# The attention output projection as seven block products per pair half, instead of eight

## The reference

```python
    o = ...                      # attention output of all heads, (544 tokens, 1024)
    yp = o @ w_out               # w_nsa_out, 1024 x 1024: the output projection
    xp = xp + rmsnorm(yp, norm_g[i, 1])
    fp, bp = conv_ffn(rmsnorm(xp, norm_g[i, 2]), zbuf, w_ffn_up[i], ...)

def rmsnorm(x, g):
    y = x * lax.rsqrt(jnp.mean(x * x, axis=-1, keepdims=True) + RMS_EPS)
    return y * g
```

## Time and profile before

| | |
|---|---|
| median of three runs | 2114.21 us |
| the profiled execution | 2110.09 us, span 2108.3 us, clock 0.999 |
| PE busy | 2070.4 us (98%), PEld (weight loads, beside PE) 1635.3 us |
| DVE / ACT / POOL busy | 1316.8 / 638.5 / 264.1 us |

### The profile page before, as it was taken

The page is one execution under the profiler, slowest core; times in us unless marked ns, Lnnn a source line. Parts: engine busy times, 40 slices in busy tenths (PEclk is TensorE's granted clock), DMA queues, the critical chain, the costliest instruction groups (busy, mean ns, idle before and its releaser), DMA issues.

```text
span 2108.3 us, 30368 instructions
## 1 busy us (share of the span) xinstructions
PE 2070.4 (98%) x11142; PEld 1635.3 (78%) x11142; DVE 1316.8 (62%) x3052; ACT 638.5 (30%) x1462; POOL 264.1 (13%) x499
## 2 busy tenths in 40 slices
PE   8999999999999999999999999999999999999998
PEld 7556777777788888888888775778888888888887
DVE  5257996672877776778323784655877777675223
ACT  3016886562332222221001321543322222220002
POOL 1002000000022222221000100410222222210001
PEclk9999999999999999999999999999999999999999
DMA  9228106994222222222221334252222222212223
GB/s 221 59 62 272 53 2 161 278 255 79 81 80 80 80 80 80 81 84 90 87 80 60 134 82 100 77 157 86 83 81 85 88 88 91 88 62 80 80 80 117
DMA packets 207493, 214.14 MB, mean 102 GB/s; under 512 B 40530, under 2 KB 192314, under 8 KB 206834
## 3 DMA queue, kind: packets, MB, share of 16 engines
q1 hardware_dynamic: 203330, 194.44, 32.0%
q0 software_dynamic: 4016, 17.75, 2.5%
HBM read 198.56 MB, written 21.93 MB: 105 GB/s over the span
## 4 chain that ended last, share of the span: by engine, by line
PE 91%; DVE 3%; SPq 2%; ACT 2%; DMA 2%; issue 1%; DVEq 0%; ACTq 0%
PE PS L2981 58%; PE PS L1847 3%; PE PS L2813 2%; PE PS L1639 2%; PE PS L2792 2%; PE PS L1718 2%; PE PS L750 2%; PE PS L822 2%; PE PS L737 2%; PE PS L2943 2%; PE PS L770 2%; PE PS L1591 2%; PE PS L2822 1%; PE PS L2716 1%; DMA arena<-in_cache_nsa_kv 1%
## 5 line engine op out<-in xcount | busy, mean ns | idle before, releaser
L2981 PE MATMUL PS<-HT,ring 128*128 128x272 f32 x1536 | 373.4, 393 | 2.3 <-DVE HT L3759 2.3
L2981 PE MATMUL PS<-arena,ring 128*128 128x272 f32 x1392 | 341.6, 392 | 0.0
L2981 PEld LDWEIGHTS PS<-HT,ring 128*128 128x128 f32 x1536 | 291.4, 190 | 63.2 <-ACT arena L3271 1.8
L2981 PEld LDWEIGHTS PS<-arena,ring 128*128 128x128 f32 x1392 | 264.3, 190 | 54.5
L3339 ACT ACTIVATE arena<-arena,CB,CW 128x560 f32<-128x560 f32 x128 | 109.1, 854 | 378.1 <-DVE arena L3819 313.9
L2981 PE MATMUL PS<-arena,CONST 128*128 128x272 f32 x768 | 191.7, 392 | 0.0
L2981 PE MATMUL PS<-arena 128*128 128x272 f32 x768 | 191.4, 392 | 0.0
L3834 DVE SCALAR_TENSOR_TENSOR arena<-arena,CW 128x560 f32<-128x560 f32 x256 | 187.3, 788 | 0.0
L2981 PEld LDWEIGHTS PS<-arena,CONST 128*128 128x128 f32 x768 | 145.9, 190 | 30.1
L2981 PEld LDWEIGHTS PS<-arena 128*128 128x128 f32 x768 | 145.8, 190 | 30.0
L4033 POOL COPY arena<-arena 128x16 f32<-128x16 f32 x128 | 50.9, 398 | 622.3 <-DVE arena L3819 524.7
(11 more groups left out here) (544 smaller groups left out, 3339.1 us busy)
## 6 DMA issues: line engine op xcount, KB each, us to landing
ring<-in_w_ffn_up SPq DMA_DIRECT2D x64, 1024.0 KB, 6.7
ring<-in_w_ffn_down SPq DMA_DIRECT2D x32, 1024.0 KB, 5.2
ring<-in_cache_nsa_kv SPq DMA_DIRECT2D x128, 128.0 KB, 5.9
arena<-in_cache_nsa_kv SPq DMA_DIRECT2D x56, 256.0 KB, 7.1
ring<-in_w_ml_in SPq DMA_DIRECT2D x12, 1024.0 KB, 6.3
arena<-in_cache_nsa_win SPq DMA_DIRECT2D x16, 512.0 KB, 6.7
out_nsa_win_sample<-in_cache_nsa_win POOLq DMA_DIRECT2D x8, 1016.0 KB, 17.4
ring<-in_w_nsa_in SPq DMA_DIRECT2D x6, 1024.0 KB, 5.8
```

The source lines that it names most:

```text
L2981: last = mm(PS[:, bank, 0:HALF], lhs[:, k, :], rhs(k), start=(first and k == 0), stop=(done and k == 3))
```

## The change

Seven of the eight pair halves of the projection are computed as seven block products. A pair half is a 2 x 2 block product: two output blocks by two quarters of 136 tokens, over two halves of the input channels. The pair half that is left plain is (half 0, pair 0), by `out_part` as before. What was 14 blocks of 8 matmuls of 272 columns is now 7 groups (half 0 with pairs 1, 2, 3, half 1 with pairs 0 to 3) of 7 products of 4 matmuls of 136 columns, in the order 1, 2, 5, 6, 7, 3, 4.

```diff
         def out_bank(idx, m):
-            return (m + 2 * (idx == 1)) % 4
+            return 2 + m % 2 if idx == 1 else m % 4
...
+            def out_group(gi):
+                h, p = A_GROUPS[gi]
+                arrived(W_AO + p)
...
+                for i, j in enumerate(A_PRODUCTS):
...
+                    n = 7 * gi + i
+                    if n in (1, 2):
...
+                    elif n < 4:
+                        pe.wait_ge(s_z, Z0[1] + (2 if n == 0 else 1))
+                    else:
+                        out_read(n - 4)
+                    if j in (5, 6, 7, 3):
+                        pe.wait_ge(s_su, ASU + A_SUMS.index((p, {5: "s1", 6: "s2", 7: "s3", 3: "s4"}[j])) + 1)
+                    if j in (5, 6, 7, 4):
+                        pe.wait_ge(s_xs, AXS + 4 * h + {5: 1, 6: 2, 7: 3, 4: 4}[j])
+                    for k in range(4):
+                        last = mm(out_place(gi, j), lhs[:, k, :], rhs[:, k, :], start=(k == 0), stop=(k == 3))
...
+                    if gi == 3 and j == 7:
+                        z_sum(1, 0, 4)
+            def out_product(ready):
+                for gi in range(7):
...
+                    out_group(gi)
+                    if gi == 5:
+                        x_gathered(2, 0, 6)
...
+            def attention_out():
+                out_chunk(1, M_AO0, 0, 0)
+                out_chunk(1, M_AO0, 0, 1)
+                out_first(0)
+                out_fifth(0)
+                for gi in (1, 2, 3):
+                    out_first(gi)
+                    out_squares(gi - 1)
+                    out_fifth(gi)
+                root(1, 0, 4)
...
+                out_first(6)
+                out_squares(5)
+                root(2, 0, 6)
+                out_fifth(6)
+                out_squares(6)
+                root(1, 1, 5)
...
+            def out_early():
+                out_tokens(0)
+                out_sums(1, ("s3", "s1", "s2", "s4"))
+            def before_first_ffn():
...
+                out_tokens(1)
+                out_adds(0, A_ADDS)
+                gather(1, 0, range(1, 2))
+                out_sums(0, ("s3", "s1"))
+                out_sums(2, ("s3", "s1", "s2", "s4"))
+                out_adds(1, A_ADDS)
...
+                gather_joined(2, 0, range(5, 8))
+                out_adds(5, A_ADDS[4:7])
+                inverse(2, 0, half(0))
+                scaled(2, 0)
+                gather(1, 1, range(4, 6))
+                out_adds(6, A_ADDS)
+                gather(1, 1, range(6, 7))
+                weight_sums(0, 0, 0)
+                inverse(1, 1, half(1))
```

More of the change, by code:

```diff
@@ L1170, in nsa_act, with nsa_dve @@
                     heads_copy(p)
-        def nsa_dve(dve, chain):
+        def nsa_dve(dve, chain, out_early):
             v = nc.vector
@@ L1457, in nsa_dve @@
                 else:
+                    out_early()
                     heads_copy(p)
@@ L2931, in out_product, with out_read @@
+            def out_read(n):
+                gi, i = divmod(n, 7)
+                j = A_PRODUCTS[i]
+                if j in (1, 5):
+                    pe.wait_ge(s_ac, AAC + 2 * gi + (1 if j == 1 else 2))
+                else:
+                    pe.wait_ge(s_ev, out_added(gi, A_READER[j]))
+            def out_product(ready):
+                for gi in range(7):
+                    if gi == 3:
                         for s, n in ready:
                             pe.wait_ge(s, n)
[L2933 to L2949, removed]
@@ L3239, in out_chunk, with out_first, out_fifth, out_squares @@
                                      scale=NG[:, 8 * idx + m:8 * idx + m + 1]).then_inc(s_z, 1)
+            def out_first(gi):
+                act.wait_ge(*out_done(gi, 1))
+                h, p = A_GROUPS[gi]
+                copy(ZT[:, 2 * p + 1, quarters(h)[1]], out_place(gi, 1)).then_inc(s_ac, 1)
+            def out_fifth(gi):
+                act.wait_ge(*out_done(gi, 5))
+                h, p = A_GROUPS[gi]
+                copy(ZT[:, 2 * p + 1, quarters(h)[0]], out_place(gi, 5)).then_inc(s_ac, 1)
+            def out_squares(gi):
+                h, p = A_GROUPS[gi]
+                for c in range(2):
+                    m = 2 * p + c
+                    act.wait_ge(s_ev, out_added(gi, ("c12", "c21")[c]))
+                    nc.scalar.activation(squared(1)[:, m, half(h)], ZT[:, m, half(h)], ACT.Square).then_inc(s_sqz, 1)
+                    nc.scalar.activation(ZT[:, m, half(h)], ZT[:, m, half(h)], ACT.Copy,
+                                         scale=NG[:, 8 + m:9 + m]).then_inc(s_z, 1)
+            def attention_out():
[8 more added lines that the diff above has]
+                root(1, 0, 4)
+                out_first(4)
+                out_squares(3)
+                out_fifth(4)
+                x_squares(2, 0, range(0, 3))
+                out_first(5)
+                x_squares(2, 0, range(3, 8))
+                out_squares(4)
+                out_fifth(5)
+                out_first(6)
[4 more added lines that the diff above has]
+                root(1, 1, 5)
+                x_squares(2, 1, range(8))
+                root(2, 1, 5)
+                state_copies(0)
             def out_copies(idx, m0):
@@ L3503, in joined_gained, with joined_runs @@
                 joined_runs(idx, cols, (6, 7))
-            def joined_runs(idx, cols, plain=()):
+            def joined_runs(idx, cols, plain=(), between=None):
                 runs = ((0, 2), (2, 4), (4, 6), (6, 7), (7, 8))
@@ new lines, in out_sums @@
+            def out_sums(p, names):
+                a11, a12, a21, a22 = slot_blocks((W_AO + p) % RING)
+                w = A_WS[p]
+                dve.wait_ge(s_w[(W_AO + p) % RING], loaded(W_AO + p))
+                for x in names:
+                    out, a_, b_, op = {"s3": (w["s3"], a11, a21, ALU.subtract), "s1": (w["s1"], a21, a22, ALU.add),
+                                       "s2": (w["s2"], w["s1"], a11, ALU.subtract),
+                                       "s4": (w["s4"], a12, w["s2"], ALU.subtract)}[x]
+                    if x in ("s2", "s4"):
+                        dve.wait_ge(s_su, ASU + A_SUMS.index((p, {"s2": "s1", "s4": "s2"}[x])) + 1)
+                    v.tensor_tensor(out, a_, b_, op).then_inc(s_su, 1)
@@ new lines, in out_adds @@
+            def out_adds(gi, names):
+                h, p = A_GROUPS[gi]
+                qa, qb = quarters(h)
+                z1, z2, u3 = ZT[:, 2 * p, :], ZT[:, 2 * p + 1, :], A_U3[gi % 2]
+                first, fifth = z2[:, qb], z2[:, qa]
+                for x in names:
+                    out, a_, j = {"c11": (z1[:, qa], first, 2), "u2": (first, first, 6), "u4": (z1[:, qb], first, None),
+                                  "u3": (u3, first, 7), "c22": (first, u3, None), "c12": (z1[:, qb], z1[:, qb], 3),
+                                  "c21": (fifth, u3, 4)}[x]
+                    if j is not None:
+                        dve.wait_ge(*out_done(gi, j))
+                    if x == "c11":
+                        dve.wait_ge(s_ac, AAC + 2 * gi + 1)
+                    elif x == "u4":
+                        dve.wait_ge(s_ac, AAC + 2 * gi + 2)
+                    if x in ("u4", "u3", "c22", "c12", "c21"):
+                        dve.wait_ge(s_ev, out_added(gi, {"u4": "u2", "u3": "u2", "c22": "u3", "c12": "u4", "c21": "c22"}[x]))
+                    v.tensor_tensor(out, a_, fifth if j is None else out_place(gi, j), ALU.add).then_inc(s_ev, 1)
@@ L3956, in _ @@
             project()
-            nsa_dve(dve, chain)
+            nsa_dve(dve, chain, out_early)
             dve.wait_ge(s_kvo, 16 * (1 + 2 * NB))
-            before_ffn(0)
+            before_first_ffn()
             ffn(0)
```

87 lines of the change are left out of this document (78 added, 9 removed).

## The result

| | before | changed |
|---|---|---|
| median | 2113.75 us (5 runs) | 2122.52 us (5 runs, 2120.80 to 2124.09) |
| ratio | | 1.0044, 95% interval 1.0033 to 1.0055 |
| profiled execution | 2110.09 us, span 2108.3 | 2124.09 us, span 2122.3 |
| mean granted clock of it | 0.999 | 0.995 |

The change makes the kernel slower by 8.8 us by the medians. The time of 2122.52 lies in the forecast range, 2.5 us above the forecast of 2120.0; the change itself is 3.0 us above the forecast +5.8. The two profiled executions are 14.0 us apart, more than the medians: the changed one happened to have more of the half clock, also in places that the change doesn't touch. So what follows takes waits and spacings from the profiles, and totals from the runs.

The account below looks back on a forecast made before the run. PE, 91% of the last chain, bounds the kernel. Start 498.5, columns 45.5, norms 1.4 and waits end at 555.6 against 550.79, +4.8; with 0.85 behind, +5.8 taken: 2120.0 us on median 2114.2, range 2114.5 to 2125.0.

Parts of the forecast that it names:

- The columns: PE's 392 records of 136 columns at 0.116 us spacing take 45.5 us, saving 5.8 us at most.
- The rival of 0.12 to 0.125: Weight loads set the projection's record spacing, or the half clock comes: 2121 to 2124 us; chance 20% together.
- The start: PE's first product waits for ACT's scaled copy in bank 3 and starts at 498.5: 2.0 us lost.
- The eight early sums: `out_early` on DVE, some 5.4 us, fits into its idle time from 490.30 to 496.6 and costs nothing.
- The early waits: PE waits for DVE's sums before product 5: 1.7 us in group 1, 0.9 in group 2, 0.1 one product later.
- Group 5, and `x_gathered`: PE waits 0.7 us for `c12` before group 5's product 5, then 1.5 us for DVE before `x_gathered`.
- The last group: In group 6, product 3 waits for `c11` behind root, reciprocal, `scaled` and gathers: 5.1 us lost.
- The rival of half the waits: Waits are half as long, 2.6 us or less in group 6: +1 to +3, about 2116 us; chance 24%.
- After the last product: Half 1's mean square first needs an add and a gather: done 2.05 us after the last product, 0.85 more.
- The sum of the path: Start, columns, norms and waits through the projection, plus the later mean square: +5.8 us in all.
- The clock: PE's clock may halve in group 6's long wait: 1 to 2 us more, kept in the range, not the sum.
- the slow rival: Projection products slower than 0.116 us spacing, or the clock falls: 2121 to 2124 us; chance 20%.

Follow-up runs that it names:

- E1: Changed kernel with its products rotated by one bank, so the first goes to a free bank; 2120.27 us, ratio to before 1.0034.
- E8: Kernel before with one wait added: TensorE's third block waits until ACT has copied the second; 2115.09 us, ratio 1.0010.
- E10: E6 with `x_gathered`, and ACT's root behind it, one block later; 2108.36 us, ratio to before 0.9982.
- E3: Changed kernel with the weight sums of pairs 2 and 3 formed earlier on DVE, between the adds of the group before; 2119.14 us, ratio to before 1.0028.
- E2: Changed kernel, last group reordered: ACT's root right behind group 5, adds spread between reciprocal and pairs of `scaled`; 2117.40 us, ratio to before 1.0025.
- E4: Changed kernel with ten unread matmuls of 272 columns in a free bank before product 3 of the last group; 2121.02 us, ratio to before 1.0041.
- E7: Changed kernel with only `c11`, the last group's first add, moved ahead of the second reciprocal on DVE; 2119.96 us, ratio to before 1.0036.
- E5: Changed kernel with the edits of E1, E2 and E3 together; 2113.40 us, ratio to before 1.0002.
- E6: Block products only for half 0's three pair halves, half 1 plain as before, banks and sums as in E1 and E3; 2110.78 us, ratio to before 0.9990.
- E9: E10 with a fourth group of block products, (half 1, pair 0); 2109.16 us, ratio to before 0.9988.
- E11: Kernel before with only `x_gathered` and the root behind it one block later, no block products; 2110.90 us, ratio 0.9998.

## Why the prediction was right, and where it was short

- **The columns.** The spacing of 0.116 that it took from 129 columns is what was measured. It lies on the slope of the columns and above the 0.111 of loads alone, so nothing shows the weight loads setting it. The rival of 0.12 to 0.125 fell.
- **The start.** 2.0 lost, measured 1.91 in the bracket; E1 removes it and E8 alone makes it. Right. The eight early sums cost nothing, as forecast: DVE does them from 492.71 to 498.10, ahead of the heads' turn, and the start of the path in E10 shows no loss.
- **The early waits.** 1.7, and 0.9 and 0.1 one product later: measured 1.47, 0.74. The names of the releasers on PE are "issue" here; that they are DVE's sums is shown by E3, where the sums come sooner and the waits are gone. Right, each about 0.2 too high.
- **Group 5, and `x_gathered`.** 0.7 and 1.5: measured 0.40 and 1.40. Right in kind, the first 0.3 too high. In the working, 527.1 + 15.8 is 542.9 and not the 543.2 written there; the stretch of 15.8 measured 548.01 + 1.39 - 533.03 = 16.4.
- **The last group.** 5.1 (553.6 - 548.6 is 5.0) by a chain of root, reciprocal, `scaled`, gathers, `c11`: measured 4.97, with ACT and DVE in that order. E2 gives the size of the whole (3.9 of path). The rival of half the waits fell.
- **After the last product.** 2.05 after it, 0.85 more than before. The changed profile has the half clock in this place; at full clock, in E4, 559.78 + 1.18 - 557.95 - 1.09 = 1.92 from the end of the last product's row to that of the mean square's, and before 550.62 + 1.38 - 550.79 = 1.21. So 0.7 more. Right, 0.1 too high.
- **The sum of the path.** +5.8, measured +6.0. Most of its waits came out a little smaller as brackets, and the sum a little larger; a wait costs more than its bracket (last section).
- **The clock.** This is the step that was short. The prediction saw that the clock could fall in the wait of 5 us and priced it at 1 to 2 us, but left it out of the sum, at a chance of 20% together with slower records. It did fall, in the wait itself, and cost 1.87 us. A second fall was not foreseen: the start wait of 1.9 us was followed by one too, which cost 1.66 us in the changed kernel's profile. E4's, E7's and E8's have it as well, E2's and E3's not: there the same wait was followed by full clock. In the mean over the runs the term is estimated at 3.7 us (the rest of the first row of the table), against 2.8 (6.1 x 0.46) by the slope within kernels and 6.1 at most, its whole lost clock. The time of 2122.52 falls where the slow rival stood, by the forecast's own walk plus that rival's clock.
- **Luck in the number.** The forecast stood on 2114.2, the median of three runs, where 27 others have a mean of 2112.9. The change is +8.8 by the medians and +9.7 by the means, for a forecast of +5.8, so 1.3 us of what the sum lacked was made up by a base that was too high.

What stays open: how much of the 3.7 us belongs to the two waits, and how much to stretches elsewhere that change from execution to execution. Of the half clock in the changed kernel's profile, the stretches at 18, 397 and 493 us lie ahead of the changed work. E4, with the long wait filled, has 3.8 us less lost clock than the changed kernel, and E2, where it is gone, 4.0 less; but E3, which keeps the long wait and falls in it in its profile, has 3.7 less as well. So the runs show that the kernels with long waits lose more clock than the kernel before, but not which wait each us belongs to. The profiles show the place: half clock directly behind the heads' turn stands in four of the six kernels with the start wait and in none of the seven without it, and half clock in the last group or at the mean square behind it in all four with the wait of 5 us and in none of the other nine. A filling of the start wait was not tried.

The Trainium skill, "TensorE: Matmul & The Clock Gate", Part 1, has the throttled state as the default and activity as what releases it. For the wait of 5 us the traces of the changed kernel, E1, E3 and E7 agree, each with the half clock in it or right behind it (6.8, 6.8, 3.4 and 6.8 us long). For the wait of 1.9 us they agree in four profiles and not in E2's and E3's.

## What to carry to other kernels

Fewer columns pay where the engines that feed and empty them have idle time: in half 0, in front of 9.00 us of DVE's idle time, each group was worth its 0.84 us, while the four groups of half 1 together, where DVE waited 1.78 and 1.05 us, gave nothing even with the waits reordered away (path -1.2 in E5, -1.9 in E6). As written, all seven groups cost 9 us. One group of half 1 alone (E9) did shorten the path by 1.0, but its runs don't show a gain. So put such a scheme where the helper engine is idle, and leave the stretch plain in which its queue leads to the next norm. Move a chain, not the instruction that PE is seen to wait for (E7), and put a new wait of PE into the sum with the clock that it can bring, not beside it.

## What the runs showed of the hardware

- **A wait costs more than its bracket.** In E11 the brackets of 0.25 and 0.69 us are gone, and the two pieces around them became 0.38 and 0.95 shorter (523.32 - 497.52 = 25.80 against 522.62 - 496.44 = 26.18, and 550.37 - 524.24 = 26.13 against 550.62 - 523.54 = 27.08). From the heads' turn to the first product it is 2.24 us in E2, with a bracket of 1.92, and 0.17 in E5, without one: 2.07.
- **The half clock is partly chance.** The kernel before had a mean clock of 1.000 to 0.995 in single executions and ran from 2109.53 to 2117.51 us. One and the same wait of 1.9 us was followed by the half clock in four profiles and not in two (E2, E3).
